# The high part of a weight tile: one instruction of 2048 columns in place of two of 1024

## The reference

```python
hl  = rmsnorm(x, norm1_w) * (1.0 + sc1) + sh1
out_l, _, _ = token_mixer(hl, s_f, s_b, grid, lp)          # ... hyena and SSD branches @ w_out
x = x + g1 * out_l
hl2 = rmsnorm(x, norm2_w) * (1.0 + sc2) + sh2
x = x + g2 * (jnp.square(jax.nn.relu(hl2 @ w_mlp1)) @ w_mlp2)
...
def peer_ffn(h, w_q, subkeys, u_tab, v_tab):               # last layer of the second block
    ...
    u = u_tab[i_]
    a = jax.nn.gelu(jnp.einsum('td,tkd->tk', x_, u), approximate=False)
    return jnp.einsum('tk,tkd->td', a * g_, v_tab[i_])
```

## Time and profile before

| | us |
|---|---|
| median of three runs | 4454.16 |
| lowest and highest | 4451.92 and 4454.51 |
| the profiled execution | 4445.12 |
| its span | 4443.3 |
| PE busy | 4263.6 (96%) |
| POOL busy | 3526.2 (79%) |
| DVE busy | 2521.2 (57%) |
| ACT busy | 1751.7 (39%) |
| mean granted clock of PE | 0.981 |

### The profile page before, as it was taken

The page is one execution under the profiler, slowest core; times in us unless marked ns, Lnnn a source line. Parts: engine busy times, 40 slices in busy tenths (PEclk is TensorE's granted clock), DMA queues, the critical chain, the costliest instruction groups (busy, mean ns, idle before and its releaser), DMA issues.

```text
span 4443.3 us, 66434 instructions
## 1 busy us (share of the span) xinstructions
PE 4263.6 (96%) x24570; PEld 3665.0 (82%) x24570; DVE 2521.2 (57%) x3903; ACT 1751.7 (39%) x1979; POOL 3526.2 (79%) x2700
## 2 busy tenths in 40 slices
PE   7999898998999999999999899999999999999999
PEld 5778687487888888888888788899888888888887
DVE  7852366634332335544323432788867957875794
ACT  3333443244444444443344343543334333333333
POOL 5754898067888988888789777988988898898897
PEclk9999999899999999999999999999999999999999
DMA  8743678034555555445455444444554454454443
GB/s 349 297 154 137 257 298 301 7 142 164 188 180 188 189 182 177 161 161 178 161 199 190 162 160 150 173 171 162 188 179 172 173 190 171 162 189 180 171 171 142
DMA packets 116177, 813.73 MB, mean 183 GB/s; under 512 B 13463, under 2 KB 17848, under 8 KB 19000
## 3 DMA queue, kind: packets, MB, share of 16 engines
q1 hardware_dynamic: 108720, 787.30, 48.8%
q10 hardware_dynamic: 7240, 23.30, 1.5%
HBM read 804.26 MB, written 6.29 MB: 182 GB/s over the span
## 4 chain that ended last, share of the span: by engine, by line
PE 58%; POOL 26%; issue 8%; DVE 7%; ACT 1%; POOLq 0%; DVEq 0%; ACTq 0%
PE psum L543 29%; POOL w_lo L464 20%; PE psum L547 15%; POOL ada_acc L494 6%; PE psum L532 1%; PE psum L533 1%; PE psum L534 1%; DVE out_hl L3127 1%; DVE out_hl L3125 1%; DVE hid L3123 1%; PE psum L1297 1%; PE psum L679 1%; PE psum L849 1%; PE psum L680 1%; PE psum L681 1%
## 5 line engine op out<-in xcount | busy, mean ns | idle before, releaser
L464 POOL TENSOR_TENSOR w_lo<-ring,w_hi 128x512 fp32r<-128x512 f32 x2416 | 3121.0, 1316 | 674.4 <-ACT w_hi L1373 652.2
L1373 ACT ACTIVATE w_hi<-ring 128x1024 fp32r<-128x1024 f32 x1228 | 1292.1, 1060 | 1923.6 <-PE psum L547 1662.6
L543 PE MATMUL psum<-hc_hl,w_hi 128*128 128x512 f32 x5120 | 1312.2, 398 | 33.8 <-DVE hc_hl L2007 10.0
L543 PEld LDWEIGHTS psum<-hc_hl,w_hi 128*128 128x128 f32 x5120 | 925.1, 190 | 213.5 <-issue 16.9
L547 PEld LDWEIGHTS psum<-hc_hl,w_lo 128*128 128x128 f32 x5120 | 700.2, 191 | 52.8 <-POOL w_lo L464 1.5
L547 PE MATMUL psum<-hc_hl,w_lo 128*128 128x256 f32 x5120 | 715.2, 283 | 1.1 <-POOL w_lo L464 1.1
L543 PE MATMUL psum<-out_hl,w_hi 128*128 128x512 f32 x2048 | 519.8, 396 | 16.7 <-DVE x L3137 14.0
L543 PEld LDWEIGHTS psum<-out_hl,w_hi 128*128 128x128 f32 x2048 | 372.6, 191 | 84.9 <-DVE x L3137 14.6
L494 POOL TENSOR_TENSOR ada_acc<-ada_acc,ada_row 128x512 f32<-128x512 f32 x224 | 288.7, 1319 | 27.7 <-ACT ada_row L1530 20.5
L547 PEld LDWEIGHTS psum<-out_hl,w_lo 128*128 128x128 f32 x2048 | 282.8, 193 | 20.3
L547 PE MATMUL psum<-out_hl,w_lo 128*128 128x256 f32 x2048 | 288.6, 284 | 0.0
(11 more groups left out here) (467 smaller groups left out, 5402.9 us busy)
## 6 DMA issues: line engine op xcount, KB each, us to landing
ring<-stream SPq DMA_DIRECT2D x620, 1024.0 KB, 4.8
ring<-mixed SPq DMA_DIRECT2D x96, 1024.0 KB, 6.3
ada_in<-ada SPq DMA_DIRECT2D x32, 1024.0 KB, 7.1
kv_dram<-kv_out ACTq DMA_DIRECT2D x32, 128.0 KB, 4.9
x<-x ACTq DMA_DIRECT2D x2, 2048.0 KB, 10.3
kv<-kv_dram ACTq DMA_DIRECT2D x2, 2048.0 KB, 7.9
mem_raw<-mem ACTq DMA_DIRECT2D x1, 2048.0 KB, 8.3
ctx_raw<-ctx ACTq DMA_DIRECT2D x1, 2048.0 KB, 12.3
```

The source lines that it names most:

```text
L464: m = pool.tensor_tensor(w_lo[:, slot, c:c + 4], ring[:, s, h * KC // 2 + c:h * KC // 2 + c + 4], w_hi[:, slot, c:c + 4].bitcast(F32), ALU ...
L543: pe.matmul(psum[:, b, :].rearrange("p (s t) -> p s t", s=2), w_hi[:, slot, c], x_hl[c], start=start(c), stop=False, skip_group_check=True)
L1373: act.activation(w_hi[:, 2 * (s % 2) + h], ring[:, s, k], ACT.Copy).then_inc(hi_ready, 1)
```

## The change

`split_tile` no longer calls `split_half` twice. It issues one ACT instruction over the whole tile (128x2048), to the two neighbouring slots of `w_hi` at once. Before it, ACT waits until PE has done both halves of tile g - 2 (`half_done` at 2g - 2), and after it `hi_ready` rises by 2 in one step. All that goes through `split_tile` is changed: 468 tiles, 936 of the 1228 instructions of L1373. The other 292 (252 of them in the MLP) go on calling `split_half`. POOL, PE, DVE and SP run the same instructions in the same order. Lines behind the change have a number one higher.

```diff
         def split_tile(g, turn, s):
             act.wait_ge(landed[s], turn * 16 + 16)
-            split_half(g, s, 0)
-            split_half(g, s, 1)
+            act.wait_ge(half_done, g * 2 - 2)
+            act.activation(w_hi[:, 2 * (s % 2):2 * (s % 2) + 2].rearrange("p h k n -> p (h k) n"), ring[:, s],
+                           ACT.Copy).then_inc(hi_ready, 2)
```

## The result

The changed kernel takes 4471.15 us (median of 6 runs, 4468.38 to 4473.48), the kernel before on the same chip and beside it 4452.77 (6 runs, 4448.4 to 4454.51). The ratio is 1.0043, 95% interval 1.003 to 1.0055: slower, 4471 was forecast.

The account below looks back on a forecast made before the run. PE, busy 96%, was taken to bound the kernel, its waits mostly on DVE. Terms summed to 17.1 us, added to the median 4454.16: 4471.3, so 4471; 8 in 10 range 4456 to 4488.

Parts of the forecast that it names:

- Steady stages: Stages paced by PE: low parts come 3.6 us later, but 2.7 of 6.3 in hand remain, so cost 0.
- Bursts in kv: Two places in kv with nothing ahead: the first signal comes 0.84 us later each time, +1.7.
- Start of dil: ACT's square root at dil's start comes 0.84 us later, and POOL's block as much again: +1.6.
- POOL against DVE: Each microsecond of POOL moved into stretches where DVE holds PE costs 0.67 us, by a lock; DVE terms 14.0.
- Start of pq: POOL's last block of o would lie over the second four L2619, taking 4.79 instead of 2.71: +2.0, bounds 0 to 2.1.
- Starts of q and peer: Same price with 0.5 to 1 us of POOL at each start: +0.9 together, bounds 0 to 2.1.
- First quarter's end: End of the first expert quarter's up part: POOL's block ends near 3104.9, not 3101.24: +2.5, bounds 0.9 to 3.7.
- The other three: Ends of the other three expert quarters: POOL busy 2.3 us more in each stretch, +4.6, bounds 0 to 8.
- A: Experiments' theory: POOL's later low parts stand over DVE's work where DVE holds PE; for e1 +10 to +16 us.
- only the first signals count: Rival: POOL's shift evens out or DVE's slack hides it, so only 3.1 us remain: 4457, chance 0.23.
- The faster one: Rival: POOL thins out in the DVE-bound stretches, so the DVE terms turn their sign: 4443, chance 0.07.
- The third: Rival, much slower: the 0.9 us in hand at `half` is used up and 32 tiles wait: 4487, chance 0.13.

Follow-up runs that it names:

- e3: The change only in steady stretches, 180 of the 468 tiles, halves elsewhere: 4445.64 us, ratio 0.9995 to the kernel before.
- e4: The complement: whole-tile instruction at the other 288 tiles, halves in the steady stretches: 4465.64 us, ratio 1.004 to the kernel before, +17.6.
- e1: Changed kernel with two ACT instructions a tile again, each signalled by itself, both behind the later wait: 4469.54 us, ratio 1.0048 to the kernel before.
- e5: Kernel before with POOL's subtraction cut from 512 to 32 columns, all waits, signals and loads kept: 4370.94 us, ratio 0.983 to the kernel before.
- e6: Changed kernel with POOL's subtraction cut from 512 to 32 columns, all waits, signals and loads kept: 4376.72 us, 5.8 over e5.
- e9: Kernel before with POOL working in pieces of 1024 columns instead of 512 at the four expert quarter ends: 4476.74 us, ratio 1.0064, +26.3.
- e7: Kernel before with POOL working in pieces of 256 columns instead of 512 at the four expert quarter ends: 4423.46 us, ratio 0.9942, -23.5.
- e2: Two ACT instructions a tile with the kernel before's waits, but both halves signalled together after the second: 4462.91 us, ratio 1.0031 to the kernel before.
- e8: Changed kernel with POOL working in pieces of 256 columns at the four expert quarter ends: 4447.22 us, 23.8 over e7.
- e10: e7 plus pieces of 256 for stream tiles 28 to 35, br_dil and out2's first four tiles: 4421.21 us, ratio 0.9937 to the kernel before.

## Why the prediction was right

The time, 4471 forecast and 4471.15 measured, is closer than the terms are. By its own steps, against the table:

- Steady stages, 0: right, 2.6 in hand where I had 2.7, and e3 shows that it costs nothing.
- Bursts in kv, +1.7: 1.5 in e4, 1.0 in the trace after, where 0.5 had been lost at the first tile. The cause is the late signal, by the length: e1 has 0.
- Start of dil, +1.6: 1.7.
- POOL against DVE: the mechanism is right (e5, e6, e9), as is the lock over shared bandwidth. Its price of 0.67 was taken from lengths that e7 and e9 reproduce by the size of POOL's instruction. Its parts are where I erred. End of kv +2.5: 2.7. br_dil +1.5: 1.3. Start of pq +2.0: 3.7, above my bound of 2.1; I had the 2.2 on DVE but not the granted clock, which was 0.72 around and behind PE's new wait. Starts of q and peer +0.9: 3.2 (0.5 and 2.7), above the 2.1 I had given as bound; of the 2.7, PE's wait on DVE's L2025 is 0.9 and one on L3070 is 0.5, and the rest are longer matmuls. First quarter's end +2.5: 0.3, below my bound of 0.9; POOL's block did end 3.6 later relative to PE, but DVE got an instruction through in a gap of 0.30 between two blocks (3108.17). The other three +4.6: 6.7, as -0.3, +3.5 and +3.5.
- The 0.5 between mixing and ret and the 1.7 behind the last expert matmul, I hadn't.

So the mechanism was right and the hit to a microsecond was luck, twice over. My terms add up to 17.1, and the two traces differ by 23.3; for the profiled execution I had 4462.2, and it took 4468.38. And I added the 17.1 to the median of three runs, 4454.16, all from the upper of the two groups of the last section; the runs of before beside the experiments have medians from 4446.91 to 4450.47.

The quarter ends show why such terms can't be had to the microsecond. At the ends of quarters 2 and 3 in the same trace the same instructions meet POOL's blocks a little differently. POOL's start and DVE's addition in quarter 2:

```profile
3476.07 5.71 POOL L464 TENSOR_TENSOR w_lo<-ring,w_hi 128x512 fp32r<-128x512 f32 x4 [0.73 <-ACT w_hi L1378]
...
3476.05 0.42 DVE L3124 TENSOR_TENSOR hid<-before,gates 128x256 f32<-128x256 f32 x1
...
3508.01 2.83 PE L543 MATMUL psum<-out_hl,w_hi 128*128 128x512 f32 x8 [3.78 <-DVE x L3138]
```

and in quarter 3:

```profile
3857.55 5.41 POOL L464 TENSOR_TENSOR w_lo<-ring,w_hi 128x512 fp32r<-128x512 f32 x4 [0.63 <-ACT w_hi L1378]
...
3857.63 1.49 DVE L3124 TENSOR_TENSOR hid<-before,gates 128x256 f32<-128x256 f32 x1
...
3892.61 3.78 PE L543 MATMUL psum<-out_hl,w_hi 128*128 128x512 f32 x8 [7.51 <-DVE x L3138]
```

An addition that starts 0.02 before POOL passes in 0.42; one that starts 0.08 behind it takes 1.49. Up to there the two stretches had run alike to within 0.1 us. From there they part, and PE waits 3.78 in one and 7.51 in the other. It is no chance of the moment: quarter 4 repeats quarter 3 instruction for instruction. The rate of 0.67 is a mean over such meetings, and over- and underestimates partly cancelled in my sum. This may also be why e1 and e2 differ, which delay the low parts alike: by the table e1 loses 8 us more at the ends of the quarters (10.6 against 2.6), and e2 5 us more in kv and xbc. A's estimate for e1 took the terms as proportional. That ACT's hold-up isn't the cause of the difference is borne out by e6, where it costs 0.0 at the quarter ends; that it is the phase is argued only, since no run varies the phase by itself.

The rivals: "only the first signals count" gave 3.1, and it is near what is left once POOL is taken away (5.8 in e6). The faster one falls, as POOL's busy time in the stretch rose. The third, that the time in hand is used up, didn't come in this kernel, where PE's waits for POOL stayed at 3.0 us, but did in e8.

## What to carry to other kernels

Merging two instructions of a feeder with idle time bought nothing here and took time in hand from everyone behind it. Ask what else the late work will stand over, at each place where the last wait is another engine's. Where VectorE holds the end and GpSimd works beside it, look at the length of GpSimd's instructions first: here halving them in the critical stretches gave more (-0.6%) than the change lost (+0.4%). Halving them costs time in hand, so the two must be tuned together.

## What the runs showed that I had not expected

**Wider shadow.** With POOL's subtractions cut to a sixteenth (POOL is busy for 23% of the span in place of 79%) the kernel before is 76 us, 1.7%, faster, though POOL's results are hardly ever late. DVE's busy time falls from 2521.2 to 2120.1 us with the same instructions.

**A starved instruction.** In the traces of e7, e9 and e10, one DVE instruction in dil takes 8.7 us; in the trace before it took 1.28. e7 (DVE, POOL, PE), then before:

```profile
2045.39 8.72 DVE L2808 TENSOR_SCALAR dil_s<-dil_s,dil_n 128x384 f32<-128x384 f32 x1
...
2043.87 9.96 POOL L464 TENSOR_TENSOR w_lo<-ring,w_hi 128x512 fp32r<-128x512 f32 x8
...
2054.17 0.55 PE L1123 MATMUL psum<-const,dil_s 128*128 128x128 f32 x3 [4.22 <-DVE dil_s L2808]
```

```profile
2044.18 1.28 DVE L2803 TENSOR_SCALAR dil_s<-dil_s,dil_n 128x384 f32<-128x384 f32 x1
```

It ends 0.28 behind the end of POOL's block (2053.83), so it seems to have let nearly seven of POOL's instructions go first, where others wait for one. It made dil 6.1 us longer in those three traces. The code up to there is the same in e7, e9 and the kernel before, so it hangs on the moment as well. The runs of the kernel before lie in two groups, about 4442 to 4447 and 4448 to 4454, some 6 us apart; the starved instruction would explain this, but no run shows it, since only one of them has a profile. In the trace after it took 0.48, and the runs of the changed kernel lie within 5 us; in e3, which also makes whole tiles there, it took 0.48 too, and all 11 runs lie in the lower group (4444.56 to 4448.06). So part of what the medians and the traces differ by (18.4 and 23.3) may be the kernel before meeting this and the changed one not.
